# A down-projection by seven block products in place of eight, with weight differences formed by adding transfers

## The reference

```python
def conv_ffn(h, w_up, w_conv, b_conv, w_down):
    u = h @ w_up
    ...
    a, g = jnp.split(u, 2, axis=-1)
    return (a * jax.nn.silu(g)) @ w_down
...
    x = x + gt2 * conv_ffn(h2, w_up, w_conv, b_conv, w_down)
```

## Time and profile before

| | before |
|---|---|
| median of 3 runs | 970.99 us (970.53 to 971.38) |
| the profiled execution, from first to last instruction | 968.6 us |
| PE busy | 952.3 us, 98% |
| DVE, ACT, POOL busy | 603.2, 434.7, 503.9 us |
| granted clock of TensorE, mean | 1.000 |
| up-projection's last matmul starts | 814.10 us |
| down-projection, first to last matmul | 814.28 to 964.69 us |

### The profile page before, as it was taken

The page is one execution under the profiler, slowest core; times in us unless marked ns, Lnnn a source line. Parts: engine busy times, 40 slices in busy tenths (PEclk is TensorE's granted clock), DMA queues, the critical chain, the costliest instruction groups (busy, mean ns, idle before and its releaser), DMA issues.

```text
span 968.6 us, 18808 instructions
## 1 busy us (share of the span) xinstructions
PE 952.3 (98%) x7513; PEld 866.9 (89%) x7513; DVE 603.2 (62%) x1087; ACT 434.7 (45%) x683; POOL 503.9 (52%) x361
## 2 busy tenths in 40 slices
PE   6999999999999999999999999999999999999998
PEld 5799899977888899999987999999999999888886
DVE  6508359963575769434937998777777778903002
ACT  5244165523766564342404465555555556511110
POOL 1386723323332317772724378888888885433331
PEclk9999999999999999999999999999999999999999
DMA  9896222126011133888641313222222222322331
GB/s 335 270 157 97 78 76 55 58 77 185 23 30 38 45 86 100 265 251 296 236 152 44 88 45 87 88 86 84 82 83 82 83 83 72 121 81 82 105 107 55
DMA packets 127826, 108.20 MB, mean 112 GB/s; under 512 B 8342, under 2 KB 104571, under 8 KB 127483
## 3 DMA queue, kind: packets, MB, share of 16 engines
q1 hardware_dynamic: 122728, 99.81, 34.1%
q0 software_dynamic: 1696, 3.25, 2.3%
q10 hardware_dynamic: 3315, 3.94, 1.1%
HBM read 101.45 MB, written 4.47 MB: 109 GB/s over the span
## 4 chain that ended last, share of the span: by engine, by line
PE 87%; DVE 5%; SPq 2%; issue 2%; POOL 1%; ACT 1%; DMA 1%; DVEq 0%; POOLq 0%; ACTq 0%
PE PA L1649 6%; PE PA L1647 6%; PE PA L1648 6%; PE PJ L923 6%; PE PJ L928 5%; PE PJ L924 5%; PE PA L1533 3%; PE PA L1535 3%; PE PA L1534 3%; PE PJ L1533 3%; PE PJ L1535 3%; PE PJ L1534 3%; PE PJ L1441 2%; PE PA L1367 2%; PE PJ L1442 2%
## 5 line engine op out<-in xcount | busy, mean ns | idle before, releaser
L713 POOL TENSOR_TENSOR wlo<-wraw,whi 128x1024 fp32r<-128x1024 f32 x53 | 133.1, 2513 | 257.4 <-ACT whi L1704 167.4
L923 PE MATMUL PJ<-h_hi,whi 128*128 128x320 f32 x336 | 104.8, 320 | 0.1
L924 PE MATMUL PJ<-h_lo,whi 128*128 128x320 f32 x336 | 101.1, 309 | 0.0
L928 PE MATMUL PJ<-h_hi,wlo 128*128 128x320 f32 x336 | 76.5, 309 | 0.0
L1704 ACT ACTIVATE whi<-wraw 128x1024 fp32r<-128x1024 f32 x39 | 41.0, 1052 | 71.8 <-PE PJ L928 23.2
L923 PEld LDWEIGHTS PJ<-h_hi,whi 128*128 128x128 f32 x336 | 63.0, 188 | 5.8 <-issue 3.6
L2220 ACT ACTIVATE whi<-wraw 128x1024 fp32r<-128x1024 f32 x21 | 22.3, 1060 | 98.6 <-PE PA L1535 51.6
L924 PEld LDWEIGHTS PJ<-h_lo,whi 128*128 128x128 f32 x336 | 63.1, 188 | 0.0
L880 POOL TENSOR_TENSOR behind<-behind_val,behind 128x512 fp32r<-128x512 f32 x40 | 52.0, 1301 | 19.0 <-ACT behind L2199 19.0
L1649 PE MATMUL PA<-h_hi,behind 128*128 128x320 f32 x192 | 59.3, 309 | 0.0
L928 PEld LDWEIGHTS PJ<-h_hi,wlo 128*128 128x128 f32 x336 | 56.1, 188 | 0.0
(11 more groups left out here) (593 smaller groups left out, 3234.3 us busy)
## 6 DMA issues: line engine op xcount, KB each, us to landing
wraw<-in_w_in_dram SPq DMA_DIRECT2D x72, 256.0 KB, 3.2
ada_rest<-in_w_ada_dram SPq DMA_DIRECT2D x32, 512.0 KB, 6.1
wraw<-in_w_up_dram SPq DMA_DIRECT2D x48, 256.0 KB, 3.8
wraw<-in_w_down_dram SPq DMA_DIRECT2D x42, 256.0 KB, 3.0
raw_even<-in_w_up_dram SPq DMA_DIRECT2D x40, 256.0 KB, 3.6
ada<-in_w_ada_dram SPq DMA_DIRECT2D x16, 512.0 KB, 7.5
out_dram<-x ACTq DMA_DIRECT2D x10, 256.0 KB, 2.1
x_rows<-in_x_sample_dram SPq DMA_DIRECT2D x2, 1024.0 KB, 6.5
```

The costliest lines, as they stand in the source:

```text
L713: pool.tensor_tensor(wlo[:, slot, 0:k, :], wraw[:, slot, 0:k, :], whi[:, slot, 0:k, :].bitcast(F32), ALU.subtract).then_inc(lo_done, done)
L923: pe.matmul(out, whi[:, slot, w0 + k, :], hi(k)[:, tok], start=start and k == k0, stop=False)
L924: pe.matmul(out, whi[:, slot, w0 + k, :], lo(k)[:, tok], start=False, stop=False)
L928: mm = pe.matmul(out, wlo[:, slot, w0 + k, :], hi(k)[:, tok], start=False, stop=stop and k == k1 - 1)
```

## The change

The weights' rows are paired: row block k with row block k + 11, for k from 0 to 10. With the two column halves this gives four units of 512 columns for each pair (0 and 1: row block k, near and far columns; 2 and 3: row block k + 11). The 512 latent tokens are split into a near and a far half of 256. The latent part is then made by seven block products in place of eight. The context tile has its four products as before.

- Part one, n = 0 to 10: P1, P2, P3 (two tiles of 128 tokens each) and the context tile C with all four units, 30 matmuls a pair. Part two, n = 11 to 21: P5, P7, P6, P4 on sums of activations and sums of weights, 24 matmuls a pair; pairs 0 to 9 with the four products in turn, the last one product by product in the order P6, P7, P5, P4.
- Far low weights of part one, and the low part of unit 1 in part two, come from an adding transfer: ACT writes the negated high part, and a transfer issued by POOL adds the weights to it (`landing_low`).
- Differences of the far weights of row blocks k and k + 11 are formed during the up-projection: SP loads row block q, ACT negates it, POOL issues an adding transfer, SP stores the result to `ahead_dram`, and part two loads it from there. 11 cycles have this.
- The other weight sums of part two are made by DVE in place in the raw buffer (`weight_sums`). There are three sets of high and low weights (`W_SETS`) and two raw buffers (`d_raw`).
- The convolution of the last block has its own place (`conv_of`) and is made by DVE and ACT while part one runs.
- The results are combined by ACT (`taken_out`), POOL (`merged` and the operations after it) and DVE, and stored from SP.

```diff
@@ sync engine
+                q = j - FIRST_AHEAD - 2
+                if 0 <= q < KH:
+                    sp.wait_ge(ahead_sum[q % 2], AHEAD_SUM[q % 2] + 16 * (q // 2 + 1))
+                    sp.dma_start(ahead_dram[q], d_ahead[q % 3][:, :, :]).then_inc(ahead_stored[q % 3], 16)
+                q = j - FIRST_AHEAD
...
+                    sp.dma_start(d_ahead[q % 3][:, :, :], w_dn_v[:, q, :].rearrange("p (c n) -> p c n", c=2)).then_inc(ahead_in[q % 3], 16)
+            def down_rows(n):
...
+                elif n - 2 < KH:
+                    sp.wait_ge(hi_done, H_DOWN + 3 * (n - 2) + 2)
+                    sp.wait_ge(actlo_set, PART_LOW["weight", n - 2])
+                else:
+                    sp.wait_ge(actlo_set, PART_LOW["far", n - 2 - KH])
...
+                for h in range(2):
+                    rows = w_dn_v[:, n % KH + KH * h, :].rearrange("p (c n) -> p c n", c=2) if h or n < KH else ahead_dram[n - KH]
+                    sp.dma_start(d_raw[n % 2][:, 2 * h:2 * h + 2, :], rows).then_inc(raw_in[n % 2 ^ 1], 16)
@@ gpsimd
             for c in CYCLES:
+                q = c - FIRST_AHEAD
+                if 0 <= q < KH:
+                    pool.wait_ge(ahead_neg, 1 + q + 1)
+                    pool.dma_start(d_ahead[q % 3][:, :, :], ahead_rows(q), accum_op=ALU.add).then_inc(ahead_sum[q % 2], 16)
                 unit_low(c, "A12")
...
+            def landing_low(n):
...
+                pool.dma_start(out, rows, accum_op=ALU.add).then_inc(low_landed[n % W_SETS], 16)
@@ tensor
+            for n in range(KH):
...
+                for i in range(2):
+                    mm = down(d_bank("P1", i), tile_of(a_hi[slot][:, 0, :], i), tile_of(a_lo[slot][:, 0, :], i), n, 0, n == 0, last)
...
+                for c in range(2):
+                    mm = down(d_bank("C", c), tile_of(t_hi, 0), tile_of(t_lo, 0), n, c, n == 0, False)
+                mm.then_inc(dn_ps, 1)
+                pe.wait_ge(low_landed[n % W_SETS], landed_low(n))
...
+            for k in range(KH - N_LAST):
+                for p, name in enumerate(("P5", "P7", "P6", "P4")):
+                    sum_ready(name, k)
...
+            for name in D_LAST:
+                for i in range(2):
+                    for k in range(KH - N_LAST, KH):
@@ scalar
                 if m == NF - 1:
+                    down_high(0, 0)
+                    down_high(0, 1)
+                    down_rows_high(0)
...
                 if m < NF:
                     first_tap(m, 1)
                 unit_high(m + 1, "S4", "P3")
+                ahead_negative(m - FIRST_AHEAD + 1)
+                if m == NF - 1:
+                    act.wait_ge(lo_done, L_DOWN)
+                    down_negative(0)
+                    down_high(1, 0)
...
+            for k in range(2, KH):
+                first_half(KH + k)
+                sums_high(k)
+                down_high(KH + k, 1)
@@ vector
+                if c == NF - 1:
+                    third(0)
+                    weight_low(0)
+                    rows_low(0)
+                near_sum("C21", c, "P4", ug[:, near], ug[:, near])
...
+            def weight_sums(k):
+
+                n = KH + k
+                raw = d_raw[n % 2]
+                dve.wait_ge(raw_in[n % 2 ^ 1], raw_down(n))
+                dve.tensor_tensor(raw[:, 3, :], raw[:, 3, :], raw[:, 0, :], ALU.subtract).then_inc(sum_set, 1)
+                dve.wait_ge(sum_set, T_DOWN + 2 * k + 1)
+                dve.tensor_tensor(raw[:, 2, :], raw[:, 2, :], raw[:, 3, :], ALU.subtract).then_inc(sum_set, 1)
...
+            for k in range(1, KH):
+                weight_low(KH + k)
+                sums_low(k)
+                if 2 <= k < 6:
+                    context_out((k - 2) // 2, k % 2)
+                if k + 1 < KH:
+                    weight_sums(k + 1)
+                far_low_units(k)
...
+            for i in range(2):
+                dve.tensor_tensor(kept(0, i), kept(0, i), as_rows(product_at("P6", i)), ALU.add).then_inc(y_set, 1)
+            for i in range(2):
+                ps = product_at("P7", i)
...
+                dve.tensor_tensor(e0_[:, i, :], u3_[:, i, :], g_near, ALU.mult).then_inc(y_set, 1)
+                dve.tensor_tensor(e1_[:, i, :], u3_[:, i, :], g_far, ALU.mult).then_inc(y_set, 1)
```

More of the change, by code:

```diff
@@ new lines, in _ @@
+            for i in range(2):
+                pool.wait_ge(y_set, 6 + 3 * i + 2)
+                x_ = x2[:, 2 + i, 0:BANK]
+                pool.tensor_tensor(x_, x_, d_raw[1][:, i, :], ALU.add).then_inc(pooled_set, 1)
+            for i in range(2):
+                pool.wait_ge(y_set, 14 + i + 1)
+                pool.wait_ge(pooled_set, P_DOWN + 6 + 3 * i + 3)
+                x_ = x2[:, i, BANK:D]
+                pool.tensor_tensor(x_, x_, d_raw[1][:, 2 + i, :], ALU.add).then_inc(pooled_set, 1)
@@ L1660, in _, with down @@
                 product("P2", j, None)
[L1662 to L1681, removed]
+            def down(out, x_hi, x_lo, n, unit, start, stop):
+                w_hi, w_lo = d_hi[n % W_SETS][:, unit, :], d_low(n, unit)
+                pe.matmul(out, x_hi, w_hi, start=start, stop=False)
+                pe.matmul(out, x_hi, w_lo, start=False, stop=False)
+                return pe.matmul(out, x_lo, w_hi, start=False, stop=stop)
@@ L2171, in first_tap @@
                 u, first = (ug, NF) if b else (ua[:, j % 2, :], 0)
[L2172 removed]
+                act.activation(conv_of(j), u[:, 1:1 + n_], ACT.Identity, scale=tap(1, j + V_W1 + first), bias=tap(2, j + first))\
                    .then_inc(tap_set, 1)
@@ new lines, in _ @@
+            first_half(KH)
+            down_high(KH, 1)
+            sums_high(0)
+            for i in range(2):
+                taken_out(kept(0, i), "P1", i, D_FIRST["P1"])
+            first_half(KH + 1)
+            for i in range(2):
+                taken_out(as_rows(ev2[:, i, :]), "P2", i, D_FIRST["P2"])
+            taken_out(as_rows(ev_c[:, 0, :]), "C", 0, D_FIRST["C0"])
+            for i in range(2):
+                taken_out(kept(8, i), "P3", i, D_FIRST["P3"])
+            taken_out(as_rows(ev_c[:, 1, :]), "C", 1, None)
@@ L2306, in _ @@
+            down_high(KH + 1, 1)
+            sums_high(1)
+            for k in range(2, KH):
+                first_half(KH + k)
+                sums_high(k)
+                down_high(KH + k, 1)
             act.wait_ge(stored, 2 * 16 + 16 * 2 * NT)
@@ new lines, in _ @@
+            first_of(0)
+            third(1)
+            second_fourth(1)
+            weight_low(1)
+            rows_low(1)
+            last_low(1)
+            first_of(1)
+            fourth_low(1)
+            early_low(0)
+            conv(NF - 1, 1)
+            conv(NF - 1, 0)
+            gate_product(NF - 1)
+            for k in range(2, KH):
+                third(k)
+                early_low(k - 1)
+                second_fourth(k)
+                weight_low(k)
+                rows_low(k)
+                last_low(k)
+                first_of(k)
+                fourth_low(k)
```

500 lines of the change are left out of this document (376 added, 124 removed).

## The result

The changed kernel takes 1014.9 us (median of 4 runs, 1013.89 to 1016.08) against 970.76 before (969.56 to 971.38): a ratio of 1.0454, 95% interval 1.0439 to 1.0469, 44.1 us slower. The profiled execution, the longest of the four, has a span of 1014.2 us, 45.6 more than the 968.6 of the earlier trace rows.

The account below looks back on a forecast made before the run. The prediction took PE's stream of matmuls as the bound, with a longer ring in part two. Terms -15.8 + 2.9 + 5.5 + 19.0 + 9.7 = +21.3 on 970.99 gave 992.3 us, range 973 to 1012.

Parts of the forecast that it names:

- the ring of part two: Part two: load, weight sums and far low parts wait on each other, so loads run one after another, 8.1 us apart.
- L: Part two: time from the issue of a pair's first 512 KB load to the landing of its second, taken as 5.4 us.
- Matmuls: Down-projection: 594 matmuls in place of 660, 0.2267 us each, and the old stage's gaps gone: -15.8 us.
- Up-projection: Ring of waits between POOL, ACT and DVE grows 0.58 us to 12.72 in 11 cycles: +2.9 us, bounds 0 and 5.6.
- First matmul: Start of the down-projection: DVE's added work delays the first matmul from 814.28 to 815.7 us, 1.5 of the start's +5.5.
- First accumulate: Start of the down-projection: PE waits 4.0 us after 12 matmuls for POOL's first accumulating transfer; start in all +5.5 us.
- Part two: Second part of the down-projection: ring longer than PE's work makes PE late by 9L - 29.6, +19.0 us.
- End: After PE's last matmul: POOL's dependent operations decide, +8.2, with 1.5 for stretched DVE adds: +9.7 us, bounds 7 and 13.
- A: Rival: PE stays the bound to its last matmul, no supply late, only the tail is paid: 964.9 us, chance 0.06.
- B: Rival: part two's ring doesn't hold, an order being misread, the other costs stand: 973.3 us, chance 0.07.
- C: Rival: 512 KB accumulates take over 6.80 us and part one goes at their pace; at 10 us, 1027 us; chance 0.09.
- D: Rival: PE, idle 2.7 of 8.1 us in part two, is granted 1.2 instead of 2.4 GHz: 1011 us, chance 0.04.

Follow-up runs that it names:

- e4: The changed kernel without POOL's eleven accumulating transfers beside the up-projection; 1009.80 us.
- x3: The changed kernel without ACT's eleven negations beside the up-projection, POOL's accumulating transfers kept; 1015.78 us.
- e6: The changed kernel with part one's eleven 512 KB transfers by POOL as plain loads in place of accumulating ones; 1013.71 us.
- e2: The changed kernel with the first pair's far low part made by one POOL subtraction in place of negation and accumulating transfer; 1012.34 us.
- c0: e1's order (also for pair 0), with the first two pairs' far low parts made by POOL subtractions; 988.50 us.
- x1: c0 with the last row block's convolution moved on the vector and scalar engines from behind pair 1 to pairs 3 and 4; 987.16 us.
- e1: The changed kernel with part two's far low parts of pair k put ahead of the weight sums of pair k+1 on the vector engine; 989.80 us.
- e5: The changed kernel without part two's eleven accumulating transfers of 256 KB, P7 waiting for ACT's negation instead; 1005.72 us.
- x2: e1 without POOL's ten last operations, the vector engine's 18 kept; 983.95 us.

## Why the prediction was wrong in size and right in kind

The direction and the four places stood as forecast, and so did the ring of part two; the time of 992.3 is 22.6 us short and the range ended at 1012, 2.9 us too low. **The step that failed is the term of part two: "For L: ... I take the middle, 5.4: +19.0 us"**. L was 6.9 us and the term 30.9. With it failed, for the same reason, the first accumulate's landing, 9.1 us in place of at most 4.4. Point by point:

- **Matmuls**, -15.8: right, 66 fewer at 0.2267.
- **Up-projection**, +2.9: 5.2 (e4: 5.1 us won without the issue). The ring grew by 0.8 us, not 0.58, since the issue costs POOL 1.2 us and not the 0.95 of the earlier trace rows: that is the case of the upper bound, 5.6. That ACT's negation has the same price was wrong: alone it lengthens the ring by 0.34 (e4, 12.48), and beside the issue by nothing (x3).
- **First matmul**, +1.5 of the term for the start: measured 1.5.
- **First accumulate**, wait 4.0: measured 8.66, and 2.6 us more of part one, mostly 11 matmuls at the lower level of the clock. "Lands 3.9 to 4.4 us after its issue if it is as a plain load" took landings from the kernel's beginning, where the DMA engines' share was 0.60 (window 40 to 46), for a moment when it is 0.86; e6's plain load took 6.9 there, the add makes it 9.1. The bound of 7 us was too low. "From the second pair on nothing" was right for this kernel, but only because the long wait gave the others time (e2, c0, x1).
- **Part two**, +19.0: measured 30.9. The ring holds, and "from the third pair on" too. L from the turn of 9.60 is 6.9, not 5.4, and 9L - 29.6 gives 32.5. e1 shows that the ring is the cause, and e5 that L would have been 4.8 without the accumulate, under my 5.4. The formula is not confirmed by e5, for which it gives 13.6 where part two is 20.2 over its matmuls: it takes all nine turns as equal, and e5's first was not. The prediction had written "here POOL's accumulate of 256 KB runs beside" and then took the middle of rows in which no accumulate runs beside. Its own second sentence from the Trainium skill (twice the bytes, L nearer 6.1, sum 998) pointed the right way; the other, 4.4 us for 1 MB, was nearly met by two pairs of e5, 4.5 and 4.6 us, and by none of the changed kernel (6.6 to 8.0).
- **End**, +9.7: measured 12.5. "POOL decides" was wrong: the vector engine ends 1.9 us later. Stretching was put at 1.5 us; x2 shows that it is 7.1 on the vector engine's operations and 5.9 in time. The bound of 13 held; the one of "7 with no stretching" doesn't fit the sum beside it, which has 8.2 without any.

2.3 (up-projection) + 7.3 (start) + 11.9 + 2.8 = 24.3 us above the forecast sum of +21.3 make the 45.6 of the span. The high ends of all terms had been added up to 1014 in the text, and the range was cut off at 1012: the terms that share a cause (traffic and the add) reached or passed their high ends together, and a range from independent terms does not see that.

**Rivals.** A and B did not come: PE's waits for `d_far` are there. C's condition came true and its effect did not: part one's accumulates took a median of 8.9 us, over 6.80, and PE waited for the first alone. From the third on POOL issues them 5.6 to 7.7 us apart, so that two are under way at times, and the price is their rate and not their landing; the rival had treated them as one after another. D came in part: 35 matmuls of part two start 0.42 or 0.43 us ahead of the next, 7.0 us more than at 0.2267, and the granted clock is 0.83 to 0.91 (windows of 20 us from 920 on). PE is not in the ring, so most of that probably shortens its waits, which no run tests; in e1, where PE hardly waits, 7 matmuls of part two are slow.

**A version that beats both kernels was not found.** The best that computes everything, x1, is 16.2 us slower than before (18.8 in its profiled execution). What that one still pays: 6.9 up to the first matmul, 6.6 in part one (3.0 of waiting, the rest mostly at the lower clock), some 8 in part two, most of it waiting for the near units' accumulates, and 12.6 at the end, 34.5, against 15.8 won. A third raw buffer, and sums of part two without the transfers ahead, were not tried.

## What to carry to other kernels

Where two buffers are filled and emptied by one in-order engine, look whether the step that frees the one stands behind a wait for the other: then the second buffer gives nothing; here a swap of two steps was worth 25.1 us, and the 66 fewer matmuls, with the old gaps, 15.8. Price a transfer from rows of the same traffic, and an accumulating one at nearly twice its bytes, for itself and for the loads beside it. When several costs in a sum hang on one unknown, their high ends come together, and the range should be made of that case.

## What the runs showed of the hardware that was not expected

- An accumulating transfer of 512 KB took 1.96 times the DMA engines' time of a plain one in its place (e6) for each byte, 1.75 times that of the plain loads beside it, and one of 256 KB lengthened the landings of 512 KB loads beside it from 4.7 to 6.3 us. Its issue reads 0.86 us on POOL where the plain one reads 0.53 at the same place (e6).
- In POOL's rows the operation behind a transfer's issue starts 0.80 us after the issue's start, although the issue is drawn 1.16 to 1.30 us long. The other 0.4 is in the operations behind it, drawn 1.7 us long in place of 1.3 up to POOL's next wait, and what waits for their results comes that much later: the issue costs 1.2 us.
- A POOL operation and a vector operation with two SBUF inputs, 1.29 and 0.65 us alone, take some 1.7 us each side by side, so moving 10 of 28 operations to POOL won nothing (990.15 and 989.80 us).
- Behind a wait of 8.66 us PE's matmuls followed each other at 0.43 us, the pace of 1.2 GHz, for 11 matmuls; behind waits of about 2 us in part two some came slow, others not.
